# Gate/up and down projections of a SwiGLU FFN as 2x2x2 block products with seven half-size products for eight, in two phases, on Trainium2

## The chip, the cores and the metric

The kernel runs on one core of a Trainium2 chip. The metric is the device time of one execution in microseconds; the time of a kernel is the median of several runs. A profile is one execution recorded by the hardware profiler. Its engines are TensorE (PE; its weight loads are PEld), VectorE (DVE), ScalarE (ACT), GpSimd (POOL) and SyncE (SP), which issues all DMAs here.

## The reference

A hybrid decoder block on x of 1024 tokens by 1024 channels, all in fp32. The change touches only the FFN, with F = 2816:

```python
h = rmsnorm(x, g_ffn[i])
gu = h @ w_gate_up[i]                                   # (1024, 1024) @ (1024, 5632)
x = x + (jax.nn.silu(gu[..., :D_FF]) * gu[..., D_FF:]) @ w_down[i]   # @ (2816, 1024)
gate = jax.nn.sigmoid(rmsnorm(x, g_ple_gate[i]) @ w_ple_gate[i])
e = rmsnorm(p[i] @ w_ple_up[i], g_ple_post[i])
x = x + gate * e
```

Before the FFN come an RMSNorm, an input projection, a convolution branch and a pooling branch, and an output projection that is added to x; after the gate comes a final RMSNorm.

## The kernel before

**Precision.** Every fp32 operand of a matmul is split into a high part (a copy in the type fp32r) and a low part (the value minus the high part). A product of a 128x128 stationary tile with a 128x512 moving tile is three matmuls (`product`, L883 to L885): low by high, high by low, high by high, accumulated in one PSUM bank. ScalarE makes the high parts (`copy`, L579), GpSimd (L379) or VectorE (L1192) the low parts.

**Layout.** `xres` holds x as eight token tiles of 128x1024. For the FFN each tile is normalised (`normed`, L1210), turned by TensorE (`turn`, L919), and split into `act_hi` and `act_lo`, channels on the partitions, tokens along the free axis.

**FFN.** F is taken in 11 chunks of 256 columns. Per chunk TensorE computes gate and up for 2 stripes of 128 features and 2 halves of 512 tokens (64 products, k over 8 channel tiles), then down for 8 token tiles and 2 halves of 512 output columns (32 products). Between them `inner` makes silu(gate) * up: ScalarE a sigmoid (L817), VectorE two multiplications (L1354, L1358), ScalarE the high and VectorE the low part. `add_rows` (L1369) adds each finished down bank onto `xres`, which stays in SBUF all the time. The weights of a chunk come by three DMAs of 1 MB: two of gate/up in runs of 1 KB, one of W_down in runs of 4 KB.

**Order.** Each engine's instructions run in the order written; engines wait for each other only on semaphores, written out by hand. So an instruction that waits holds back all behind it on its engine. SyncE too waits, then issues, in written order. PSUM has 8 banks of 128x512 fp32; gate/up uses banks 0 to 3, down 4 to 7.

**Around the FFN.** The last output-projection rows (`rows_out`, tiles 4 to 7) alternate on TensorE with the turns of the normalised tiles; each tile goes `add_x` (L1305), square on ScalarE (L594), `rms` on GpSimd (L373, L376), `normed`, `turn`, split. After the FFN the same path is run for norm 2, then `gate_rows` multiplies by w_ple_gate, whose rows are loaded and split in the last chunk.

Of the kernel before, what the change touches and what calls it, by code (L numbers as in the profile page):

```python
# [19 lines left out]

# [10 lines left out]
P = 128  # L31
EPS = 1e-6
BANK = 512
HEADPAD = 16
DMA = 16


def hybrid_block(nc, x, p, g_mix, w_in, conv_w, conv_b, ln_g, ln_b, pool_w, pool_scale, w_out,
# [8 lines left out]
    TT = SEQ // P  # L47
# [5 lines left out]
    NCH = F // (2 * P)  # L53
    PAD = TAPS - 1
# [13 lines left out]
    e_dram = nc.dram_tensor("e_scratch", (TT, P, D), F32, kind="Internal").ap()  # L68

    with ExitStack() as ctx:  # L70
        def sb(name, shape, dt=F32):
            return ctx.enter_context(nc.sbuf_tensor(name, shape, dt))
# [36 lines left out]

        def cols_of(w, m):  # L110
# [31 lines left out]
        wd_hi = sem("wd_hi")  # L142
        wd_lo = sem("wd_lo")
# [39 lines left out]
        wo_used = sem("wo_used")  # L183
# [29 lines left out]
        PG_BANK = (4, 6, 2)  # L213
# [52 lines left out]
        def _(sp):  # L266
# [57 lines left out]
            load_gain(g_ffn[0])  # L324
            sp.wait_ge(w_lo, GU0)
            load_cols(w_gu_v, 0, F)
            for t in range(2, TT):
                sp.wait_ge(rows_added, 2 * (t - 1))
                load_x(t, raw_b[:, t % 2, :])
            sp.wait_ge(rows_added, 2 * TT)  # L330
            sp.dma_start(raw_b[:, :, :], w_dn_v[:, 0:2, :]).then_inc(rawb_in, DMA)
            sp.wait_ge(xn_ok, 2 * TT)
            load_gain(g_ple_gate[0])
            with sp.Fori(0, NCH - 1) as i:
                sp.wait_ge(w_lo, i * 4 + (GU0 + 4))
                load_cols(w_gu_v, (i + 1) * 256, (i + 1) * 256 + F)
                sp.wait_ge(wd_lo, i * 2 + 2)
                sp.dma_start(raw_b[:, :, :], w_down[0][bass.ds((i + 1) * 256, 256), :]
                             .rearrange("(f p) n -> p f n", p=P)).then_inc(rawb_in, DMA)
            sp.wait_ge(w_lo, GU0 + 4 * NCH)  # L340
            load_rows(0, w_pg_v[:, 0:2, :])
            load_rows(1, w_pg_v[:, 2:4, :])
            def load_e(t):
                sp.dma_start(e_place(t), e_dram[t]).then_inc(e_in[t], DMA)

            load_e(0)
            load_e(1)
            sp.wait_ge(wd_lo, 2 * NCH)
            sp.dma_start(raw_b[:, 0, :], g_ple_post[0].partition_broadcast(P)).then_inc(gfin_in, DMA)
            sp.dma_start(raw_b[:, 1, :], g_final.partition_broadcast(P)).then_inc(gfin_in, DMA)  # L350
            sp.wait_ge(w_lo, GU0 + 4 * NCH + 4)
# [17 lines left out]
        def _(pool):  # L369
# [153 lines left out]

            norm_2(0)
# [4 lines left out]
            split_cols(0, GU0 + 1)  # L529
            split_cols(1, GU0 + 2)  # L530
            norm_2(TT - 1)
            split_cols(2, GU0 + 3)
            split_cols(3, GU0 + 4)

            def ffn_splits(i, last):
                for f in range(2):
                    pool.wait_ge(wd_hi, i * 2 + (f + 1))
                    lo(bs_lo[:, f, :], raw_b[:, f, :], bs_hi[:, f, :], wd_lo)
                for m in range(4):
                    if last:  # L540
                        split_row(raw, m, ws_hi[:, m, :], ws_lo[:, m, :], GU0 + 4 * NCH + m + 1)
                    else:
                        split_cols(m, i * 4 + (GU0 + 4 + m + 1))

            with pool.Fori(0, NCH - 1) as i:
                ffn_splits(i, False)
            ffn_splits(NCH - 1, True)
# [29 lines left out]
        def _(act):  # L577
# [209 lines left out]
            for t in range(4):  # L787
                square_after(t, 1, 2 * t + 2)
            for n in range(KC, 2 * KC):
                scale_shift(n)  # L790
            turned_hi(0, 1)
            turned_hi(1, 1)
            square_after(4, 1, 10)
            square_after(5, 1, 12)
            turned_hi(2, 1)
            turned_hi(3, 1)
            square_after(6, 1, 14)
            turned_hi(4, 1)
            turned_hi(5, 1)
            act.wait_ge(wo_used, 1)  # L800
            for m in range(4):
                split_cols(m, 6 * DMA)
            square_after(7, 1, 16)
            turned_hi(6, 1)
            turned_hi(7, 1)


            def ffn(i, last):
                for f in range(2):
                    act.wait_ge(rawb_in, i * DMA + 3 * DMA)  # L810
                    act.wait_ge(rows_done, i * 16 + 16)
                    copy(bs_hi[:, f, :], raw_b[:, f, :], wd_hi)
                for f in range(2):
                    for h in range(HALVES):
                        s = 2 * f + h
                        act.wait_ge(gu_mm, i * 4 + (s + 1))
                        act.activation(wide[:, 0, (s % 2) * BANK:(s % 2 + 1) * BANK], ps[:, 2 * (s % 2), :],  # L817
                                       ACT.Sigmoid).then_inc(sig_ok, 1)
                        act.wait_ge(in_ok, i * 4 + (s + 1))
                        copy(bs_hi[:, 2 + f, h * BANK:(h + 1) * BANK],  # L820
                             wide[:, 1, (s % 2) * BANK:(s % 2 + 1) * BANK], in_hi)
                    act.wait_ge(gu_mm, i * 4 + (2 * f + 2))
                    for m in (2 * f, 2 * f + 1):
                        if last:
                            split_row(m, ws_hi[:, m, :], (7 + NCH - 1) * DMA)
                        else:
                            split_cols(m, i * DMA + 7 * DMA)

            with act.Fori(0, NCH - 1) as i:
                ffn(i, False)  # L830
            ffn(NCH - 1, True)

            for t in range(TT):
                square_after(t, 2, 16 * NCH + 2 * (t + 1))
                if t >= 3:
                    turned_hi(t - 3, 2)
            act.wait_ge(rows_done, 16 * (NCH + 1))

            def pg_rows(ks):
                for k in ks:  # L840
                    act.wait_ge(raw_in[k // 2], (7 + NCH) * DMA)
                    copy(bs_hi[:, k, :], raw[:, k, :], pg_hi)

            pg_rows(range(4))
            turned_hi(TT - 3, 2)
            turned_hi(TT - 2, 2)
# [33 lines left out]
        def _(pe):  # L880
            def product(dst, w_hi_, w_lo_, m_hi, m_lo, start, stop):

                pe.matmul(dst, w_lo_, m_hi, start=start, stop=False)  # L883
                pe.matmul(dst, w_hi_, m_lo, start=False, stop=False)  # L884
                return pe.matmul(dst, w_hi_, m_hi, start=False, stop=stop)  # L885
# [211 lines left out]
            rows_out(7, range(4, KD), True, False).then_inc(wo_used, 1)  # L1097
            rows_out(7, range(4), False, True)
            pe.wait_ge(rows_added, 14)
            turn(6, 1)  # L1100


            def down(i, t):
                h = t // HT
                if t % HT == 0:
                    pe.wait_ge(in_lo, i * 4 + (3 + h))
                for d in range(2):
                    n = 2 * t + d
                    pe.wait_ge(rows_added, i * 16 + (16 + n - 3))
                    for f in range(2):  # L1110
# [332 lines left out]
```

## Time and profile before

| what | value |
|---|---|
| time, median of 3 runs (lowest, highest) | 1134.55 us (1134.23, 1134.79) |
| span of the profiled execution, first to last instruction | 1132.9 us |
| TensorE matmul busy | 1093.7 us, 97% |
| VectorE / ScalarE / GpSimd busy | 519.5 / 304.8 / 365.7 us |
| DMA | 75.73 MB, mean 67 GB/s |

The span is that of the profiled execution; it lies 1.65 us below the median of the runs. A matmul's busy time covers its pipeline, so matmuls overlap one another in it; what one costs is the distance from start to start. The slices of the page show TensorE at 9 tenths or more from the second slice to the last, but for the fifth to eighth (5, 8, 9, 5).

### The profile page before, as it was taken

How to read it: one execution, taken by the hardware profiler on the slowest of the kernel's cores; microseconds unless marked ns; L12 is line 12 of the kernel's file. 1: busy time of each engine (PE TensorE's matmuls, PEld its weight loads, DVE VectorE, ACT ScalarE, POOL GpSimd, SP SyncE). 2: the span in 40 equal slices, each digit the busy share in tenths (PEclk: the TensorE clock that was granted, in tenths of full speed). 3: DMA queues.
4: the chain of work that ended last, by engine and by line, in shares of the span. 5: the costliest groups of instructions: out<-in, count | busy, mean ns of one | idle time of the engine just before them, and what ended most of it. 6: DMA issues, size and time to landing. Idle time of an engine off the chain costs nothing.

```text
span 1132.9 us, 12791 instructions
## 1 busy us (share of the span) xinstructions
PE 1093.7 (97%) x4909; PEld 905.0 (80%) x4909; DVE 519.5 (46%) x711; ACT 304.8 (27%) x430; POOL 365.7 (32%) x271
## 2 busy tenths in 40 slices
PE   5999999589999999999999999999999999999997
PEld 4888887468888888888888888888888888888885
DVE  5699799995433223241413314142331424139544
ACT  5734267213421120111112111111211111226332
POOL 4547689411242123122112213111311311231541
PEclk8999999799999999999999999999999999999999
DMA  8221204141041203021210302121030202101311
GB/s 283 82 75 38 75 11 174 75 130 56 22 164 41 72 1 112 0 74 37 71 40 0 111 0 74 37 74 37 0 111 0 75 36 111 38 26 50 130 56 74
DMA packets 44927, 75.73 MB, mean 67 GB/s; under 512 B 1585, under 2 KB 33857, under 8 KB 44896
## 3 DMA queue, kind: packets, MB, share of 16 engines
q1 hardware_dynamic: 44896, 75.31, 19.5%
q8 instruction: 20, 0.33, 0.1%
q14 instruction: 11, 0.09, 0.0%
HBM read 66.92 MB, written 8.39 MB: 66 GB/s over the span
## 4 chain that ended last, share of the span: by engine, by line
PE 86%; DVE 6%; issue 5%; ACT 1%; POOL 1%; DMA 1%; DVEq 1%; SPq 0%; POOLq 0%; ACTq 0%
PE ps L883 28%; PE ps L885 28%; PE ps L884 28%; DVE ps L1261 2%; PE ps L919 1%; DVE act_lo L1192 1%; DVE resid L1294 1%; DMA resid<-in_x 1%; DVE act_hi L1296 1%; ACT junk L594 0%; DVEq L1259 0%; POOL wide L468 0%; DVE scr L1210 0%; PE ps L979 0%; DVE resid L1267 0%
## 5 line engine op out<-in xcount | busy, mean ns | idle before, releaser
L883 PE MATMUL ps<-act_hi,ws_lo 128*128 128x512 f32 x832 | 325.9, 392 | 3.0 <-DVE act_lo L1192 2.6
L884 PE MATMUL ps<-act_lo,ws_hi 128*128 128x512 f32 x832 | 324.8, 390 | 0.0
L885 PE MATMUL ps<-act_hi,ws_hi 128*128 128x512 f32 x832 | 324.7, 390 | 0.0
L379 POOL TENSOR_TENSOR ws_lo<-raw,ws_hi 128x1024 fp32r<-128x1024 f32 x58 | 140.6, 2442 | 414.2 <-ACT ws_hi L579 414.2
L1354 DVE TENSOR_TENSOR wide<-ps,wide 128x512 f32<-128x512 f32 x44 | 30.4, 691 | 379.4 <-ACT wide L817 379.4
L883 PEld LDWEIGHTS ps<-act_hi,ws_lo 128*128 128x128 f32 x832 | 156.8, 189 | 36.0 <-issue 3.6
L885 PEld LDWEIGHTS ps<-act_hi,ws_hi 128*128 128x128 f32 x832 | 156.8, 188 | 32.8
L884 PEld LDWEIGHTS ps<-act_lo,ws_hi 128*128 128x128 f32 x832 | 156.9, 189 | 32.4
L1369 DVE TENSOR_TENSOR resid<-resid,ps 128x512 f32<-128x512 f32 x176 | 118.3, 686 | 82.2 <-PE ps L885 80.7
L883 PE MATMUL ps<-bs_hi,bs_lo 128*128 128x512 f32 x384 | 149.9, 390 | 0.1
L885 PE MATMUL ps<-bs_hi 128*128 128x512 f32 x384 | 149.4, 389 | 0.0
L884 PE MATMUL ps<-bs_lo,bs_hi 128*128 128x512 f32 x384 | 149.4, 389 | 0.0
L1261 DVE SCALAR_TENSOR_TENSOR ps<-resid,convw,ps 128x512 f32<-128x512 f32 x184 | 122.6, 745 | 0.0
L817 ACT ACTIVATE wide<-ps 128x512 f32<-128x512 f32 x44 | 26.3, 598 | 340.4 <-PE ps L885 340.4
L379 POOL TENSOR_TENSOR bs_lo<-raw_b,bs_hi 128x1024 fp32r<-128x1024 f32 x24 | 57.0, 2396 | 144.6 <-ACT bs_hi L579 144.6
L883 PEld LDWEIGHTS ps<-bs_hi,bs_lo 128*128 128x128 f32 x384 | 72.1, 188 | 15.4 <-ACT raw_b L579 0.5
L885 PEld LDWEIGHTS ps<-bs_hi 128*128 128x128 f32 x384 | 72.1, 188 | 15.0
L884 PEld LDWEIGHTS ps<-bs_lo,bs_hi 128*128 128x128 f32 x384 | 72.1, 188 | 14.8
L579 ACT ACTIVATE bs_hi<-raw_b 128x1024 fp32r<-128x1024 f32 x24 | 24.1, 1054 | 174.4 <-PE ps L885 171.6
L883 PE MATMUL ps<-ws_hi,act_lo 128*128 128x512 f32 x136 | 54.6, 401 | 13.0 <-POOL ws_lo L379 11.4
L594 ACT ACTIVATE junk<-resid 128x1024 bf16<-128x1024 f32 (+1 forms) x33 | 34.1, 1032 | 110.4 <-DVE resid L1305 63.7
L579 ACT ACTIVATE ws_hi<-raw 128x1024 fp32r<-128x1024 f32 x60 | 60.0, 1047 | 3.4 <-PE ps L885 3.4
(114 smaller groups left out, 1193.6 us busy)
## 6 DMA issues: line engine op xcount, KB each, us to landing
raw<-in_w_gate_up SPq DMA_DIRECT2D x22, 1024.0 KB, 7.4
raw_b<-in_w_down SPq DMA_DIRECT2D x11, 1024.0 KB, 4.8
resid<-in_x SPq DMA_DIRECT2D x8, 512.0 KB, 7.2
raw<-in_w_in SPq DMA_DIRECT2D x4, 1024.0 KB, 6.6
raw<-in_w_out SPq DMA_DIRECT2D x4, 1024.0 KB, 5.7
e_scratch<-raw_b SPq DMA_DIRECT2D x8, 512.0 KB, 2.6
raw_b<-in_x SPq DMA_DIRECT2D x8, 512.0 KB, 4.4
raw<-in_w_ple_gate SPq DMA_DIRECT2D x4, 1024.0 KB, 5.9
```

The lines of the kernel that those rows point to most:

```text
L379: pool.tensor_tensor(dst, src, hi.bitcast(F32), ALU.subtract).then_inc(done, 1)
L579: act.activation(dst, src, ACT.Copy, scale=scale).then_inc(done, 1)
L594: act.activation(junk[:, c], xres[:, t, c], ACT.Square, accum_out=ss[:, at:at + 1]).then_inc(ss_ok, 1)
L817: act.activation(wide[:, 0, (s % 2) * BANK:(s % 2 + 1) * BANK], ps[:, 2 * (s % 2), :], ACT.Sigmoid).then_inc(sig_ok, 1)
L883: pe.matmul(dst, w_lo_, m_hi, start=start, stop=False)
L884: pe.matmul(dst, w_hi_, m_lo, start=False, stop=False)
L885: return pe.matmul(dst, w_hi_, m_hi, start=False, stop=stop)
L919: ins = pe.transpose(ps[:, turn_bank(norm, t) + j, q * P:(q + 1) * P], xn_place(n)[:, k * P:(k + 1) * P], ident[:, :])
L1192: dve.tensor_tensor(dst, src, hi.bitcast(F32), ALU.subtract).then_inc(done, 1)
L1261: dve.scalar_tensor_tensor(out=conv_c if k == last_odd else acc, in0=resid[:, bass.ds(c * UW + (k + h * BANK), BANK)], scalar=convw[:, bas ...
L1354: dve.tensor_tensor(wide[:, 0, a], ps[:, b, :], wide[:, 0, a], ALU.mult).then_inc(gs_ok, 1)
L1369: dve.tensor_tensor(x_, x_, ps[:, 4 + n % 4, :], ALU.add).then_inc(rows_added, 1)
```

## The change

Both FFN products are written as Winograd's form of Strassen's 2x2x2 block product, in which seven half-size products and some sums replace eight. With blocks A11..A22 and B11..B22: S1 = A21 + A22, S2 = S1 - A11, S3 = A11 - A21, S4 = A12 - S2, T1 = B12 - B11, T2 = B22 - T1, T3 = B22 - B12, T4 = B21 - T2; products 1 = A11 B11, 2 = A12 B21, 3 = S4 B22, 4 = A22 T4, 5 = S1 T1, 6 = S2 T2, 7 = S3 T3.

**Phase 1, gate/up.** The token halves are the even and the odd token tiles, the k halves channels 0 to 511 and 512 to 1023, the column halves gate and up. The S forms of the activations are made once, at the hand-over (`even_lo`, `pair_forms`, `form_hi`). F is taken in 22 quads of 128 features; each quad is 7 parts of 4 products (28). For each quad VectorE makes T1 to T4 (four 128x512 subtractions), ScalarE copies and GpSimd low parts follow, and the seven parts accumulate in two banks, out of which partial sums are copied and added:

```diff
+        HEAD = ((0, 1), (0, 2), (1, 1), (1, 2), (0, 6), (0, 5), (0, 7), (0, 3), (0, 4),
+                (1, 6), (1, 5), (1, 7), (1, 3), (1, 4))
+        ORDER = HEAD + tuple((q, i) for q in range(2, QUADS) for i in (1, 2, 6, 5, 7, 3, 4))
...
+                if i == 6:
+                    pe.wait_ge(fs2_lo, 2)
+                    pe.wait_ge(t12_lo, q + 1)
+                    pe.wait_ge(p1_ok, q + 1)
+                if i == 5:
+                    pe.wait_ge(fs1_lo, 4)
+                    pe.wait_ge(c11_ok, q + 1)
+                if i == 7:
+                    pe.wait_ge(fs34_lo, 1)
+                    pe.wait_ge(t34_lo, q + 1)
+                    pe.wait_ge(u2_ok, q + 1)
+                if i == 3:
+                    pe.wait_ge(fs34_lo, 2)
+                    pe.wait_ge(wb22_lo, q + 1)
+                    pe.wait_ge(p5_ok, q + 1)
+                if i == 4:
+                    pe.wait_ge(fa_lo, 12)
+                    pe.wait_ge(c22_ok, q + 1)
```

VectorE's loop over the quads:

```diff
+            for q in range(QUADS):
+                if q:
+                    in_1(q - 1)
+                    if q % 2 == 0:
+                        in_forms(q // 2 - 1)
+                if q >= 2:
+                    c11(q)
+                if q + 1 < QUADS:
+                    t_12(q + 1)
+                if q:
+                    gs_0(q)
+                if q + 1 < QUADS:
+                    t_34(q + 1)
+                c22(q)
+                in_0(q)
```

ScalarE's:

```diff
+            for q in range(QUADS):
+                if q:
+                    sigmoid_1(q - 1)
+                    hi_t34(q)
+                if q >= 2:
+                    copy_p1(q)
+                if q:
+                    sigmoid_0(q)
+                copy_u2(q)
+                if q and q + 1 < QUADS:
+                    hi_b(q + 1)
+                copy_p5(q)
+                if q + 1 < QUADS:
+                    hi_t12(q + 1)
+                    hi_b22(q + 1)
```

GpSimd's:

```diff
+            for q in range(QUADS):
+                lo_t34(q)
+                if q + 1 < QUADS:
+                    if q:
+                        lo_b(q + 1)
+                    lo_t12(q + 1)
+                    lo_b22(q + 1)
```

`in_forms` makes the S forms of the FFN activations of two quads; SyncE stores seven forms of 128x512 per pair of quads in DRAM (`in_dram`). `xres` holds only four tiles now: after `add_x` each x tile is stored in DRAM (`x1_dram`), and the place of the others is used for the partial sums. Weights of a quad come as two DMAs of 512 KB in runs of 512 B.

**Phase 2, down.** Seven parts in the order 1, 5, 6, 3, 7, 2, 4, each over 11 steps (one per pair of quads), 77 steps of 4 products. A step loads one activation form and one W_down block of 128x512 (256 KB each, runs of 2 KB), in parts 5 and 7 a second W_down block; ScalarE makes two high parts, VectorE two low parts and in parts 5, 6, 7 and 4 one T form. The raw ring has four places, the split ring three:

```diff
+            def step_hi(n):
+                pi, i, j = e_step(n)
+                act.wait_ge(ab_in[n % 4], 2 * DMA * (n // 4 + 1))
+                if n >= 3:
+                    act.wait_ge(ed_mm, 4 * (n - 2))
...
```

VectorE's loop over the steps:

```diff
+            for n in range(3):
+                step_lo(n)
+            in_1(QUADS - 1)
+            in_forms(PAIRS - 1)
+            for n in range(3, STEPS):
+                pi, i, j = e_step(n)
+                step_lo(n)
+                if n + 2 < STEPS and E_ORDER[(n + 2) // PAIRS] in (5, 6, 7, 4):
+                    step_t(n + 2)
+                if pi and j < 4:
+                    step_sum(pi - 1, j)
```

SyncE's queue at the change of phase:

```diff
+            for n in range(4, 7):
+                load_step(n)
+            store_pair(PAIRS - 1)
+            sp.wait_ge(d_mm, len(ORDER))
+            for form in range(7):
+                sp.wait_ge(in_stored[form], DMA * PAIRS)
+            for t in EVEN_ODD:
+                sp.dma_start(xres[:, t, :], x1_dram[t]).then_inc(x_in[t], DMA)
+            for n in range(7, STEPS):
...
+                load_step(n)
```

TensorE's steps:

```diff
+            for n in range(STEPS - 3):
+                pi, i, j = e_step(n)
+                pe.wait_ge(e_lo, 2 * n + 2)
+                if n == 0:
+                    pe.wait_ge(fa_lo, 12)
+                    pe.wait_ge(gs1_ok, QUADS)
+                    pe.wait_ge(c12_ok, QUADS)
+                if j == 0 and pi >= 2:
+                    pe.wait_ge(ed_ok, 4 * (pi - 1))
+                for m in range(4):
+                    step_mm(n, m).then_inc(ed_mm, 1)
+                if pi == 6 and j in (5, 7):
+                    turn(j // 2 - 2, 2)
+            pe.wait_ge(e_lo, 2 * STEPS)
+            for m in range(4):
+                for n in range(STEPS - 3, STEPS):
+                    last = step_mm(n, m)
+                last.then_inc(ed_mm, 1)
```

**Around them.** The last output-projection tile is done in two column halves with the turn of tile 6 between them (`last_half`); the turn of an even tile now waits for `fs4_ok` (its predecessor pair's last S form), the turn of an odd tile for `fa_lo`. The w_ple_gate rows are loaded one by one and split between steps 12 and 47 of phase 2 (high parts ScalarE, low parts GpSimd). Norm 2 and `gate_rows` take the even tiles first; two turns lie in the last part of phase 2, the other six between the gate rows.

## Rows read from the trace of the kernel before

**Rows 1.** The page: span, and busy time by engine

```profile
span 1132.9 us, 12791 instructions
...
PE 1093.7 (97%) x4909; PEld 905.0 (80%) x4909; DVE 519.5 (46%) x711; ACT 304.8 (27%) x430; POOL 365.7 (32%) x271
```

**Rows 2.** A window of 100 us in the FFN: busy us (instructions) per engine, clock, DMA

```profile
400.00:500.00 100.00, 100.00 (x443) 82.81 (x442) 30.96 (x46) 17.61 (x23) 23.82 (x10) 1.00 0.15 48
```

**Rows 3.** Timeline of SyncE's DMA issues: W_down of two successive chunks

```profile
382.62 0.37 SPq L338 DMA_DIRECT2D raw_b<-in_w_down  x1
...
447.90 0.37 SPq L338 DMA_DIRECT2D raw_b<-in_w_down  x1
```

**Rows 4.** Chain of waits, 200 longest pieces: turns of tiles 4 and 5, a stall of TensorE

```profile
296.56 1.75 PE ps L919 x16
...
1034.13 0.51 issue
```

**Rows 5.** Timeline of ScalarE in one FFN chunk: start, duration, idle before and releaser

```profile
452.73 0.60 ACT L817 ACTIVATE wide<-ps 128x512 f32<-128x512 f32 x1 [8.87 <-PE ps L885]
454.81 0.63 ACT L579 ACTIVATE bs_hi<-wide 128x512 fp32r<-128x512 f32 x1 [1.48 <-DVE wide L1358]
```

**Rows 6.** Timeline of VectorE in the same chunk

```profile
453.36 0.69 DVE L1354 TENSOR_TENSOR wide<-ps,wide 128x512 f32<-128x512 f32 x1 [10.82 <-ACT wide L817]
454.08 0.69 DVE L1358 TENSOR_TENSOR wide<-wide,ps 128x512 f32<-128x512 f32 x1
455.47 0.69 DVE L1192 TENSOR_TENSOR bs_lo<-wide,bs_hi 128x512 fp32r<-128x512 f32 x1 [0.70 <-ACT bs_hi L579]
```

**Rows 7.** Page, part 5: 1024-wide splits on GpSimd and ScalarE

```profile
L379 POOL TENSOR_TENSOR ws_lo<-raw,ws_hi 128x1024 fp32r<-128x1024 f32 x58 | 140.6, 2442 | 414.2 <-ACT ws_hi L579 414.2
...
L579 ACT ACTIVATE ws_hi<-raw 128x1024 fp32r<-128x1024 f32 x60 | 60.0, 1047 | 3.4 <-PE ps L885 3.4
```

**Rows 8.** Timeline of VectorE while GpSimd works, 180 to 184 us

```profile
180.86 2.87 DVE L1294 TENSOR_TENSOR resid<-resid 128x512 f32<-128x512 f32 x1 [0.28 <-DVE resid L1267]
```

**Rows 9.** Timeline of GpSimd in the same stretch

```profile
180.75 2.42 POOL L379 TENSOR_TENSOR ws_lo<-scr,ws_hi 128x1024 fp32r<-128x1024 f32 x1
```

**Rows 10.** Timeline of VectorE at the hand-over to the FFN, 296 to 316 us

```profile
296.60 0.69 DVE L1305 TENSOR_TENSOR resid<-ps,raw_b 128x512 f32<-128x512 f32 x1 [4.69 <-PE ps L885]
...
300.19 1.28 DVE L1210 SCALAR_TENSOR_TENSOR scr<-resid,rs,gain 128x1024 f32<-128x1024 f32 x1
...
312.87 2.63 DVE L1210 SCALAR_TENSOR_TENSOR scr<-resid,rs,gain 128x1024 f32<-128x1024 f32 x1
```

**Rows 11.** Timeline of ScalarE in the same stretch

```profile
297.32 1.06 ACT L594 ACTIVATE junk<-resid 128x1024 bf16<-128x1024 f32 x1 [9.55 <-DVE resid L1305]
```

**Rows 12.** Timeline of GpSimd in the same stretch

```profile
298.83 0.55 POOL L376 TENSOR_TENSOR rs<-ss,neg_half 128x1 f32<-128x1 f32 x1
```

**Rows 13.** DMA issues by line: KB each, median us from issue to landing

```profile
raw_b<-in_w_down SPq DMA_DIRECT2D x11, 1024.0 KB, 4.8
...
e_scratch<-raw_b SPq DMA_DIRECT2D x8, 512.0 KB, 2.6
...
out_x<-scr SPq DMA_DIRECT2D x2, 256.0 KB, 2.0
```

**Rows 14.** Windows of 1 us inside transfers: 512 B, 1 KB and 4 KB runs

```profile
13.00:14.00 1.00, 0.97 (x5) 0.57 (x4) 1.00 (x2) 0.74 (x2) 0.92 (x2) 1.00 1.17 291
367.00:368.00 1.00, 1.00 (x7) 0.81 (x6) 0.69 (x1) 0.00 (x0) 0.00 (x0) 1.00 1.05 355
385.00:386.00 1.00, 1.00 (x6) 0.84 (x5) 0.00 (x0) 0.00 (x0) 0.00 (x0) 1.00 1.06 434
```

**Rows 15.** Windows of 2 us around TensorE's idle time at 239 us

```profile
240.00:242.00 2.00, 0.00 (x0) 0.00 (x0) 2.00 (x4) 0.00 (x0) 0.00 (x0) 1.00 0.00 0
244.00:246.00 2.00, 2.00 (x12) 1.82 (x11) 2.00 (x4) 0.74 (x1) 0.00 (x0) 0.50 0.00 0
246.00:248.00 2.00, 2.00 (x10) 1.85 (x9) 2.00 (x4) 1.56 (x4) 0.93 (x3) 0.66 0.82 254
```

More of the change, by code:

```diff
@@ L21 @@
+import math
 from contextlib import ExitStack
@@ L330, in _ @@
[L330 to L339, printed above, removed]
@@ L528, in _ @@
                 norm_2(t)
-            split_cols(0, GU0 + 1)
-            split_cols(1, GU0 + 2)
+            lo_b(0)
             norm_2(TT - 1)
[L532 to L547, printed above, removed]
+            lo_b(1)
+            lo_t12(0)
+            lo_b22(0)
+            for q in range(QUADS):
[5 more added lines that the diff above has]
+                    lo_b22(q + 1)
+            for k in range(KD):
+                pool.wait_ge(pg_hi, k + 1)
+                hi_, lo_ = (ws_hi, ws_lo) if k < 4 else (bs_hi, bs_lo)
+                lo(lo_[:, k % 4, :], scr[:, k % 3, :], hi_[:, k % 4, :], pg_lo)
             def e_rms(t):
@@ L797, in _ @@
+            form_hi(3)
             square_after(6, 1, 14)
[L798 to L802, printed above, removed]
-            square_after(7, 1, 16)
[L804 to L842, printed above, removed]
@@ L844, in _ @@
-            pg_rows(range(4))
-            turned_hi(TT - 3, 2)
-            turned_hi(TT - 2, 2)
+            hi_b(0)
+            form_hi(4)
+            form_hi(5)
+            form_hi(6)
+            hi_b(1)
+            square_after(7, 1, 16)
+            hi_t12(0)
+            hi_s2(0, 3)
+            copy_p1(0)
+            form_hi(7)
+            hi_s2(3, 4)
+            sigmoid_0(0)
+            copy_p1(1)
+            for i in (7, 3):
+                act.wait_ge(fs4_ok, 4)
+                copy(s_form(ws_hi, bs_hi, i), s3 if i == 7 else s4[:, :, :], fs34_hi)
@@ L848, in gate @@
+            for t in range(4, TT):
+                act.wait_ge(ed_ok, 25 + t - 4)
+                square(t, 2)
+                if t == 5:
+                    turned_hi(2, 2)
+            turned_hi(3, 2)
             def gate(t, j, c):
@@ L1330, in _ @@
+            even_lo(0)
             normed(2, 1, 2)
-            turned_lo(1, 1)
+            pair_forms(0)
             normed(3, 1, 2)
@@ L1334, in _ @@
             add_x(5)
-            for t in range(4, 6):
-                turned_lo(t - 2, 1)
-                normed(t, 1, 2)
+            even_lo(1)
+            normed(4, 1, 2)
+            pair_forms(1)
+            normed(5, 1, 2)
             add_x(6)
-            turned_lo(4, 1)
+            even_lo(2)
             normed(6, 1, 2)
-            turned_lo(5, 1)
+            pair_forms(2)
+            even_lo(3)
             add_x(7)
-            turned_lo(6, 1)
+            t_12(0)
             normed(7, 1, 2)
-            turned_lo(7, 1)
@@ L1376, in _ @@
[L1376 to L1391 removed]
+            s2_lo(0, 3)
@@ L1392, in _ @@
+            for m in range(4):
+                step_sum(6, m)
+            turned_lo(1, 2)
+            normed(2, 2, 3)
+            normed(3, 2, 3)
+            turned_lo(2, 2)
+            turned_lo(3, 2)
+            for t in range(4, TT):
+                normed(t, 2, 3)
+                if t >= 5:
+                    turned_lo(t - 1, 2)
             turned_lo(TT - 1, 2)
```

689 lines of the change are left out of this document (538 added, 151 removed).

## The prediction

> **What bounds the kernel now.** I read the page first: TensorE is busy for 97% of the span, VectorE for 46%, GpSimd for 32% [rows 1]. In a window of 100 us inside the FFN TensorE has no idle time at full clock, the other engines are busy 31, 18 and 24 us, and the DMA engines are at 0.15 [rows 2]. So in the FFN time is the number of matmuls times their distance. A chunk is 64 + 32 products of 3 matmuls, 288, and successive chunks are 447.90 - 382.62 = 65.28 us apart [rows 3]: 0.2267 us a matmul, 718 us for 11 chunks. Only two kinds of things can count: matmuls that go, and places where TensorE comes to wait.
>
> **What goes.** Gate/up had 11 x 64 = 704 products and gets 22 x 28 = 616; down had 352 and gets 77 x 4 = 308. That is 132 products, 396 matmuls, x 0.2267 = 89.8 us. Moving tiles stay 512 wide in three passes, so I leave the distance as it is; that phase 1 reads them as four runs of 128 is the one unknown in it. No row shows this form. Its bounds are nothing and, were such a matmul twice as long, 1848 x 0.2267 = 419 us, far above the gain; the turns' and down's 128-wide runs of `act_hi` as weights cost nothing that [rows 3] shows, so I take nothing.
>
> **Phase 1, steady state.** A part is 12 matmuls, 2.72 us, a quad 19.04. The unit prices: ScalarE 0.60 to 0.63 for 512 columns and 1.05 for 1024, VectorE 0.69 and 0.72 from start to start when chained, GpSimd 2.44 for 1024, hand-overs 0.2 from TensorE and 0.03 to 0.1 else [rows 5 to 7]. Per quad: VectorE 11 operations + half of `in_forms`, 13 x 0.70 = 9.1 us; ScalarE 3 x 1.05 + 6 x 0.61 = 6.8; GpSimd 3.5 x 2.44 = 8.5. All are under half of 19.04. What matters is the order. Counted from a quad's start: `sigmoid_1` 0.2 to 0.8, `hi_t34` to 1.85, so `lo_t34` 1.9 to 4.4; `copy_p1` 2.9 to 3.5 (part 6 wants it at 5.44); VectorE's `c11` at 5.65 (part 5 wants it at 8.16); `copy_u2` 8.4 to 9.0 (part 7: 10.9); `copy_p5` 11.1 to 11.7 (part 3: 13.6); `c22` 13.8 to 14.5 (part 4: 16.3). The tightest is an even quad, with `in_forms` ahead of `c11`.
>
> There the port question enters. An operation of VectorE with both inputs in SBUF, 0.69 us when GpSimd rests [rows 6], took 2.87 us when GpSimd ran a 2.42 us subtraction, and ended 0.56 us after it [rows 8, 9]; `normed` went from 1.28 to 2.63 in the same way [rows 10]. So the first operation of `in_forms`, at 2.3, is held until 4.9, the others follow to 7.1, `c11` ends at 7.8: 0.4 us before part 5 wants it. I take no loss here. (The Trainium skill, "SBUF — State Buffer", section "SBUF: two separate sides", calls the pair of ports shared by VectorE and GpSimd an exclusive lock held for the instruction; the trace agrees. By it the worst case would be a hold per GpSimd instruction.)
>
> **Hand-over to the FFN.** Before, TensorE did not wait here. The turns of tiles 4 and 5 end at 298.3 [rows 4], then `last_half(0)` (24 matmuls, 5.44) to 303.75. The turn of tile 6 needs the S4 of pair 2. ScalarE: square of tile 6 to 298.4 [rows 11], `hi_b(0)` to 299.5, high parts of tiles 4 and 5 to 301.5. VectorE: `even_lo(2)` to 301.2, `normed(6)`, held by `lo_b(0)` (299.5 to 301.9), to 303.2, four forms x 0.70 to 306.0: **2.3 us** late. Then `last_half(1)` to 312.4, parts (0,1), (0,2) to 317.9. `normed(7)` has its factor at 315.6 (square and `rms`, prices of [rows 11, 12]) but meets `lo_b(1)`: 318.3, **0.4** late. Parts (1,1), (1,2) to 324.6. VectorE: `s2_lo` of 1536 columns, 1.9 us, held behind `lo_t12(0)`, to 322.3, `c11` 323.0, four forms 325.8, the last S2 low part 326.5: **1.9** late. Parts 6 and 5 to 332.0; part 7 needs `t34_lo`: ScalarE has first the copies of S3 and S4 (2048 columns, 2.0 each), to 330.9, `hi_b22` and `hi_t34` to 332.5, GpSimd to 335.2: **3.3** late. Then `c22(0)` stands behind `t_12(1)` and `t_34(1)`: **0.4**. Sum 8.3 us; ends of the range 4 (no holding) and 14 (each of the SBUF-only operations held).
>
> **Change of phase.** Let T0 be the end of the last part. Step 0 waits for `gs1_ok`, the first half of `in_1(21)`, which VectorE reaches behind `in_0` (to -1.1) and six low parts (4.2): 3.1, + 0.7 = T0 + 3.9. Behind it come the second half (4.6), `in_forms` (7.5), the last store (2.0 to 2.6 to land [rows 13]; 9.9). Only then SyncE issues eight x tiles, 4.2 MB, 0.4 us each, and `load_step(7)` behind them in its queue. At 0.42 MB per us (runs of 4 KB gave 434 GB/s, of 1 KB 355 [rows 14]) that lands at 24.0; two high and two low parts, and step 7 starts at 26.0. Seven steps before it would be 19.04. So the change of phase costs **7.0 us** (3.9 at step 0, 3.1 at step 7); ends 3.9 (loads overtake) and 12 (x tiles at 291 GB/s).
>
> **Phase 2, steady state.** A step is 2.72 us of TensorE. VectorE: two low parts, in four of seven parts a T form, in four of eleven steps a sum: 3.36 x 0.70 = 2.35 us; ScalarE 1.3. A load has from the low parts of step n-4 to the T form of n: 10.88 - 5.4 = 5.5 us. 1 MB takes 4.8 us, 512 KB stored 2.6 [rows 13]; 512 KB loaded I take as 3.5 and 768 KB as 4.5 to 5. Bandwidth: 524 KB per 2.72 us is 193 GB/s, in parts 5 and 7 289 GB/s, against 355 to 434. It fits, with little room in 22 steps. Eight GpSimd low parts of 2.44, one per five steps, hold VectorE up to 2.2 us each: in parts 5 and 6 12.1 + 2.2 = 14.3 us of work per 13.6 us. TensorE has 3.1 us in hand per step. I take **3 us**; ends 0 and 22 x 0.9 = 20 (768 KB at the 219 GB/s that the lone 1 MB load shows over issue to landing: 3.6 us a step).
>
> **The end.** The last three steps wait for the low parts of step 76, whose high parts wait for step 73; `turned_lo(0)` is ahead of them on VectorE: **2.5 us**. The rest of the norms runs between gate rows of 5.44 us each and I find no wait; the 0.5 us at 1034 [rows 4] goes: 2.0. Ends 0.5 and 6.
>
> **The clock.** After 4.8 us of idle time at 239 the granted clock stood at 0.50, then 0.66, for some 3 us, that is 1.2 GHz and back to 2.4 [rows 15]: 1.5 us lost. The waits above are 2 to 4 us; after the one at step 0 the loss is hidden by step 7's wait. I take **2 us**, ends 0 and 6. (The Trainium skill, "TensorE: Matmul & The Clock Gate", "HAM oscillation — how this bites in real kernels", warns of exactly such gaps; that gaps of this size suffice no run here shows.)
>
> **Sum.** -89.8 + 8.3 + 7.0 + 3.0 + 2.0 + 2.0 = -67.5. From the profiled 1132.9 that is 1065.4, and with the 1.65 us to the median 1067.
>
> **Rivals.** (a) *Phase 2 is bound by its loads.* For it: 256 KB pieces, only four places, at most two steps under way, two thirds of the DMA capacity wanted. Against: two loads overlap, and windows inside transfers reach 355 and more. At 3.6 us a step in 22 steps the time is 1067 - 3 + 20 = 1084. The Trainium skill, "DMA: Bandwidth & Descriptors", "Bandwidth", advises transfers of at least 1 MiB; one after another, by its fit (2.0 us + bytes/436e3), two of 256 KB would be an estimated 5.2 us, far beyond a step. By rows, the store of 256 KB took 2.0 and of 512 KB 2.6 [rows 13]: the fixed part is 1.4 us, and if each load paid it alone, a step would be 2 x 2.0 = 4.0 us, x 77 - 209 = +99, which gives 1163, slower; the 2 MB of gate/up at 355 GB/s without a gap speaks against it. (b) *The port makes VectorE the bound of phase 1.* Place: nine SBUF-only operations per quad. If GpSimd's holding and its being held add up so that `c11` comes late in even quads by 1 us, 10 us: 1077. The gain is used up when a quad takes 67/22 = 3.1 us more; with all nine at 2.87 a quad is 9 x 2.87 + 4 x 0.69 = 28.6 us, +9.5, that is 1276, slower. Against: GpSimd works only 8.5 us of 19. (c) *The waits at the seams mostly vanish* (slack that I counted pessimistically): 4 + 3.9 + 0 + 0.5 gives 1053. (d) *Strided moving tiles are slower.* 3% on 1848 matmuls would be 12.6 us: 1080. Against: nothing in the rows; a weak case.
>
> **Chances.** Forecast, 1057 to 1078: 0.57. (a) in its mild form 0.14, as +99 us 0.02; (b) mild 0.10, severe 0.02; (c) 0.10; (d) 0.05. A measurement of this kernel tells 0.2%, 2.3 us, from no change. Faster 0.95, same 0.01, slower 0.04. The range takes in the forecast, (b) mild, (d), most of (a), and the near part of (c): 1054 to 1089.
>
> **What would show it.** Right: per quad 19.0 us in phase 1 with no idle TensorE; idle TensorE of about 4 us at the change of phase with `in_1` as releaser and about 3 us seven steps later, with the load of step 7 or its splits as releaser; 2 to 3 us at three places of the hand-over. Wrong: a distance over 0.2267 in phase 1; idle time per step in parts 5 and 7 released through raw's loads; VectorE operations of 2 us and more in many quads with TensorE waiting on `c11`; a clock below 1 over more than 10 us.

## The result, and the profile after

The changed kernel takes 1106.26 us (median of 4 runs, 1105.26 to 1108.31) against 1134.67 for the kernel before (4 runs, 1134.23 to 1134.95): ratio 0.9751, interval 0.9737 to 0.9764. It is 28.4 us faster, where 67.5 were forecast, and lies 17 us beyond the end of the range (1089).

The page of the changed kernel, to be read against [rows 1], and with TensorE's busy tenths, granted clock and the DMA's share in 40 slices of 27.6 us:

```profile
span 1103.6 us, 12625 instructions
...
PE 1022.3 (93%) x4513; PEld 841.0 (76%) x4513; DVE 738.2 (67%) x931; ACT 424.9 (39%) x636; POOL 426.3 (39%) x297
...
PE   5999999589987999999999999998887888999997
...
PEclk8999999799998999999999999998898998999999
DMA  8221203343203422334142324238765577643021
```

TensorE has 4909 - 4513 = 396 matmuls less, as counted, but its busy share has fallen from 97% to 93%. Four slices were thin before as well, the first, the eighth and ninth (5 and 8 tenths) and the last; the text on the profile before names the fifth to eighth, which is wrong. The others show where it fell: the 12th and 13th, the hand-over, and the 28th to the 34th, phase 2. Slices 14 to 27, phase 1, are full. Windows of 20 us, columns as in [rows 2]: two of the hand-over, one of phase 1, three of phase 2:

```profile
300.00:320.00 20.00, 16.83 (x82) 13.64 (x81) 15.18 (x17) 8.37 (x14) 7.23 (x5) 1.00 0.06 26
320.00:340.00 20.00, 13.22 (x52) 10.22 (x52) 19.90 (x19) 9.92 (x12) 7.64 (x3) 0.89 0.19 54
560.00:580.00 20.00, 20.00 (x90) 16.58 (x89) 12.63 (x15) 7.36 (x11) 8.86 (x4) 1.00 0.29 88
...
780.00:800.00 20.00, 16.15 (x59) 12.75 (x58) 14.06 (x21) 6.38 (x12) 2.35 (x1) 0.83 0.72 231
840.00:860.00 20.00, 15.91 (x58) 12.57 (x58) 9.83 (x13) 6.59 (x11) 2.36 (x1) 0.83 0.59 177
...
900.00:920.00 20.00, 14.73 (x63) 11.85 (x62) 14.24 (x22) 7.22 (x12) 2.35 (x1) 0.89 0.65 224
```

In phase 1 TensorE has no idle time; VectorE, at 63%, does not hold it up. The distance of the quads comes from TensorE's timeline, the first matmul of part 1 of quad 2 and that of quad 20:

```profile
361.79 0.39 PE L1217 MATMUL ps<-act_hi,wa_lo 128*128 128x512 f32 x1
```

```profile
704.51 0.39 PE L1217 MATMUL ps<-act_hi,wa_lo 128*128 128x512 f32 x1
```

(704.51 - 361.79) / 18 = 19.04 us a quad, 84 x 0.2267: the matmul distance of [rows 3], with moving tiles in four runs of 128 columns. So the 89.8 us of matmuls went as forecast. Part of them was given back by idle time. The view of waits for TensorE says who waited for whom (total us, times, longest); of its lines those that the kernel before does not have:

```profile
PE ps L1217 <- DVE ring_lo L1564: 29.1, 10, 5.3
...
PE ps L1217 <- POOL wc_lo L565: 5.6, 1, 5.6
...
PE ps L1217 <- DVE gtmp L1781: 3.4, 1, 3.4
...
PE ps L1263 <- DVE s L1725: 2.0, 1, 2.0
PE ps L1217 <- DVE ws_lo L1564: 1.2, 1, 1.2
```

and place by place in phase 2, TensorE's timeline (start, duration, in brackets the idle time before and its releaser):

```profile
746.12 0.77 PE L1217 MATMUL ps<-ring_hi,ring_lo 128*128 128x512 f32 x1 [3.37 <-DVE gtmp L1781]
...
771.58 0.50 PE L1217 MATMUL ps<-ring_hi,ring_lo 128*128 128x512 f32 x1 [3.44 <-DVE ring_lo L1564]
...
793.64 0.80 PE L1217 MATMUL ps<-ring_hi,ring_lo 128*128 128x512 f32 x1 [3.85 <-DVE ring_lo L1564]
```

The first is step 0, the second step 7, the other eight are one step each, and come every five steps. Behind a wait for VectorE's `ring_lo` there must be something that VectorE waits for, and that is seen in the waits of ScalarE from 740 us on:

```profile
ACT ws_hi L782 <- DMA scr<-in_w_ple_gate: 21.3, 4, 6.3
ACT bs_hi L782 <- DMA scr<-in_w_ple_gate: 20.8, 4, 7.5
```

ScalarE stood 42.1 us in eight places, 4 + 4, until a row of w_ple_gate had landed. One of them, ScalarE's timeline and SyncE's:

```profile
782.27 0.62 ACT L782 ACTIVATE ring_hi<-keep 128x512 fp32r<-128x512 f32 x1
788.95 1.06 ACT L782 ACTIVATE ws_hi<-scr 128x1024 fp32r<-128x1024 f32 x1 [6.06 <-DMA scr<-in_w_ple_gate]
789.91 0.61 ACT L782 ACTIVATE ring_hi<-raw 128x512 fp32r<-128x512 f32 x1
```

```profile
782.03 0.43 SPq L487 DMA_DIRECT2D raw<-in_w_down  x1
...
782.99 0.43 SPq L527 DMA_DIRECT2D scr<-in_w_ple_gate  x1
```

SyncE issues the row at 782.99, behind the load of step 15, which it may issue only when step 11's low parts are done. ScalarE wants it right after the high parts of step 12, at 782.9. It lands at 788.95. The high parts of step 13 stand behind it in ScalarE's queue, though step 13's loads were issued as early as 774.3 and 774.8 (they land in 3.0 and 3.8 us, median). They still need the place in the split ring that step 10 gives back; going by the 2.72 us between the earlier such moments, that was at about 784.4 (an estimate), so the row holds them for some 5.5 us. VectorE then waits for them, and TensorE, with step 12 in hand, runs dry.

Something else stands in the same wait. ScalarE makes the high part of the row first, so GpSimd starts its low part of the row just ahead of VectorE's low part of step 13. GpSimd's timeline and VectorE's:

```profile
790.08 2.35 POOL L565 TENSOR_TENSOR ws_lo<-scr,ws_hi 128x1024 fp32r<-128x1024 f32 x1 [62.03 <-ACT ws_hi L782]
```

```profile
790.56 2.43 DVE L1564 TENSOR_TENSOR ring_lo<-raw,ring_hi 128x512 fp32r<-128x512 f32 x1 [4.74 <-ACT ring_hi L782]
```

VectorE's operation, 0.68 us elsewhere, took 2.43 and ended 0.56 us after GpSimd's. In each of the eight places one low part is lengthened so, by about 1.7 us, which makes up to 13 of TensorE's 24.5 us of idle time there (an estimate: 1.7 in six places, and the whole of the two waits that are shorter than that).

**The account** in the profiled execution: 1132.9 - 89.8 + 9.95 (four waits at the hand-over: 1.99, 1.18, 1.20, 5.58) + 6.8 (steps 0 and 7) + 24.5 (eight rows: 3.85, 3.05, 1.50, 4.09, 1.10, 2.87, 2.74, 5.27) + 1.2 (the last three steps) - 0.5 (the wait of [rows 4]) = 1085.1. The span is 1103.6. The 18.5 us left are matmuls at a greater distance; the granted clock fits: its mean fell from 0.987 to 0.969, and (1 - 0.969) x 1103.6 - (1 - 0.987) x 1132.9 = 19.5 us of clock, some of it in idle time. Windows of 2 us say where: (1 - clock) x 2 us, summed, is 3.4 us at the hand-over, 5.1 between 744 and 776 us (behind steps 0 and 7), and 11.9 behind steps 13, 18, 28 and 48, together 20.4; it is nothing in phase 1, and nothing in the kernel before from 296 to 1128 us. Windows around the wait at step 13:

```profile
790.00:792.00 2.00, 0.00 (x0) 0.00 (x0) 1.44 (x1) 2.00 (x6) 1.92 (x1) 1.00 0.05 20
792.00:794.00 2.00, 0.36 (x1) 0.36 (x2) 2.00 (x3) 0.60 (x2) 0.44 (x1) 0.73 0.00 0
794.00:796.00 2.00, 2.00 (x6) 1.52 (x6) 2.00 (x5) 0.63 (x1) 0.00 (x0) 0.50 0.60 186
796.00:798.00 2.00, 2.00 (x6) 1.59 (x5) 2.00 (x4) 0.00 (x0) 0.00 (x0) 0.50 0.97 307
798.00:800.00 2.00, 2.00 (x6) 1.51 (x5) 1.10 (x3) 0.77 (x2) 0.00 (x0) 0.57 0.99 349
800.00:802.00 2.00, 2.00 (x10) 1.65 (x9) 1.79 (x3) 0.38 (x1) 0.00 (x0) 1.00 0.83 248
```

The clock is at its lower level, 1.2 GHz, for some 6 us after a wait of 3.85 us.

### The profile page after: what moved, and what is told of

Read it like the earlier page. It is cut to its first block and busy times, and to the rows that moved or that the text cites. A ratio compares the mean times of both kernels' runs of the same rounds, so it can differ in the third digit from the quotient of the medians.

```text
span 1103.6 us, 12625 instructions
## 1 busy us (share of the span) xinstructions
PE 1022.3 (93%) x4513; PEld 841.0 (76%) x4513; DVE 738.2 (67%) x931; ACT 424.9 (39%) x636; POOL 426.3 (39%) x297
## 5 line engine op out<-in xcount | busy, mean ns | idle before, releaser
L1217 PE MATMUL ps<-ring_hi,ring_lo 128*128 128x512 f32 x308 | 127.2, 413 | 32.5 <-DVE ring_lo L1564 29.1
L1564 DVE TENSOR_TENSOR ring_lo<-raw,ring_hi 128x512 fp32r<-128x512 f32 x132 | 99.7, 791 | 81.4 <-ACT ring_hi L782 81.3
L1218 PE MATMUL ps<-ring_lo,ring_hi 128*128 128x512 f32 x308 | 125.2, 406 | 0.0
L1219 PE MATMUL ps<-ring_hi 128*128 128x512 f32 x308 | 124.4, 404 | 0.0
L782 ACT ACTIVATE ring_hi<-raw 128x512 fp32r<-128x512 f32 x132 | 76.2, 622 | 103.1 <-PE ps L1219 91.0
L1217 PE MATMUL ps<-act_hi,bs_lo 128*128 128x512 f32 x240 | 93.6, 390 | 0.0
L1219 PE MATMUL ps<-act_hi,bs_hi 128*128 128x512 f32 x240 | 93.4, 389 | 0.0
L1218 PE MATMUL ps<-act_lo,bs_hi 128*128 128x512 f32 x240 | 93.4, 389 | 0.0
L1218 PEld LDWEIGHTS ps<-ring_lo,ring_hi 128*128 128x128 f32 x308 | 61.2, 199 | 12.7
L565 POOL TENSOR_TENSOR bs_lo<-raw_b,bs_hi 128x1024 fp32r<-128x1024 f32 x24 | 59.8, 2495 | 10.2 <-ACT bs_hi L782 10.2
L1217 PE MATMUL ps<-act_hi,ws_lo 128*128 128x512 f32 x128 | 51.7, 404 | 3.0 <-DVE act_lo L1564 2.6
```

The lines of the kernel that those rows point to most:

```text
L565: pool.tensor_tensor(dst, src, hi.bitcast(F32), ALU.subtract).then_inc(done, 1)
L782: act.activation(dst, src, ACT.Copy, scale=scale).then_inc(done, 1)
L1217: pe.matmul(dst, w_lo_, m_hi, start=start, stop=False, skip_group_check=onto)
L1218: pe.matmul(dst, w_hi_, m_lo, start=False, stop=False, skip_group_check=onto)
L1219: return pe.matmul(dst, w_hi_, m_hi, start=False, stop=stop, skip_group_check=onto)
L1564: dve.tensor_tensor(dst, src, hi.bitcast(F32), ALU.subtract).then_inc(done, 1)
```

## The experiments

**e1_pg_early.** Each row is issued four steps earlier:

```diff
-                if n - 4 in PG_STEP:
-                    k = PG_STEP[n - 4]
+                if n in PG_STEP:
+                    k = PG_STEP[n]
```

> The changed kernel with one edit: each w_ple_gate row is loaded four steps earlier (before the load of step n instead of step n + 4). Theory A: in the eight steps with such a row ScalarE stands in its queue until the row has landed (42 us in all in the trace of the changed kernel), TensorE runs dry for 24.5 us in eight places and restarts at half clock in five places of phase 2. Then the row's wait vanishes, TensorE's eight waits go to under 3 us in all, and the time falls from 1106 to 1068 to 1078. Theory B: the waits come from GpSimd's low parts, which hold VectorE's two-input operations (2.4 us each, as often as before): then TensorE's waits stay and the time stays within 5 us of 1106. Theory C: phase 2 is short of DMA bandwidth: the waits move to other steps, and the time stays above 1095.

1074.77 us (1073.16 to 1076.52; ratio to before 0.9481, interval 0.9465 to 0.9497), 31.5 us less than the changed kernel. In its trace ScalarE waits for no row, and of TensorE's eight waits 2.5 us are left:

```profile
771.13 0.80 PE L1217 MATMUL ps<-ring_hi,ring_lo 128*128 128x512 f32 x1 [6.18 <-DVE ring_lo L1564]
...
786.96 0.50 PE L1217 MATMUL ps<-ring_hi,ring_lo 128*128 128x512 f32 x1 [0.24 <-DVE ring_lo L1564]
...
802.17 0.50 PE L1217 MATMUL ps<-ring_hi,ring_lo 128*128 128x512 f32 x1 [1.20 <-DVE ring_lo L1564]
```

GpSimd makes the same eight low parts, and the transfers carry the same bytes. So bandwidth did not make those waits, nor did GpSimd's low parts by themselves; the rows' place in the queues did. VectorE is still held, as at step 18 in its timeline here:

```profile
798.62 2.90 DVE L1564 TENSOR_TENSOR ring_lo<-raw,ring_hi 128x512 fp32r<-128x512 f32 x1
```

Without the row's wait ahead of it, a hold of about 2 us reaches TensorE at most as the 0.2 to 1.2 us above. In the changed kernel it came on top of that wait. No run took the hold away and left the row where it was, so the two shares of the 24.5 us are read from the trace, not tested.

**e2_pg_late.** The same edit the other way (`n - 5`).

> The other way: each w_ple_gate row is loaded one step later than in the changed kernel. Theory A: each of the eight waits grows by about a step, 2.7 us, so 8 x 2.7 = 22 us more, and with the half clock after more of them 22 to 35: 1128 to 1141. Theories B and C: no change, within 5 us of 1106.

1133.62 us (1130.03 to 1136.6): 27.4 us more than the changed kernel, inside what theory A gave. ScalarE waits 60.5 us for the rows, TensorE 42.8 in the eight places. With the rows this late the whole change brings nothing: ratio to before 0.9991, interval 0.9979 to 1.0003.

**e3_fill.** Nine matmuls that add zero, ahead of five of the waits (an extract; the tile of zeros, `zt`, is written once by GpSimd at the hand-over, which is left out here):

```diff
+                if n in (13, 18, 28, 43, 48):
+                    pe.wait_ge(zt_ok, 1)
+                    pe.wait_ge(ed_ok, 4 * (pi - 1) + 1)
+                    for _ in range(9):
+                        pe.matmul(ps[:, E_BANKS[1 - E_SET[pi]][0], :], zt[:, :], act_hi[:, 0, 0:BANK],
+                                  start=False, stop=True, skip_group_check=True)
```

> The changed kernel with nine matmuls more (2.0 us) on TensorE ahead of each of five waits of phase 2 (steps 13, 18, 28, 43, 48), with a stationary tile of zeros, accumulated onto a bank whose sum is out already, so that nothing is changed by them. They lie inside waits that end no earlier for them. Theory: the half clock after a wait costs about 3 us each time at steps 13, 18, 28 and 48; with the idle time cut by 2 us it does not fall at 13, 18 and 28: 1106 to about 1097, with the same moments of landing. Rival: what follows a wait is slow for another reason, or the clock falls all the same: 1106 or up to 3 us more.

1108.41 us (1105.26 to 1110.69): no gain. At step 13 the fill did what it should, the idle time fell to 1.66 us and the clock stayed up:

```profile
792.00:794.00 2.00, 1.44 (x7) 0.86 (x5) 2.00 (x1) 2.00 (x4) 1.89 (x1) 1.00 0.00 0
794.00:796.00 2.00, 0.90 (x4) 0.77 (x5) 2.00 (x4) 0.34 (x2) 0.00 (x0) 1.00 0.00 0
796.00:798.00 2.00, 2.00 (x11) 1.64 (x10) 2.00 (x5) 0.31 (x1) 0.00 (x0) 1.00 0.83 287
```

But the next wait, at step 18, was 3.17 us in spite of its own 2 us of fill. It ended 41.0 us after step 7's start, 41.9 in the changed kernel: 0.8 us sooner, not 3; and the last wait, of step 74, ended 225.2 us after it for 223.0. At step 28 an idle time of 2.38 us was followed by 1.2 GHz all the same. At step 38 the clock fell after 2.52 us, where in the changed kernel it had not after 2.87. The windows give 10.2 us of clock from 770 us on for 13.6 in the changed kernel, 3.4 less; but fill and idle time from step 13 to step 48 come to 10.2 + 17.6 = 27.8 us for 24.5. So the experiment does not separate the clock's cost: time won by a faster TensorE in between is mostly lost again at the next wait.

**e4_gs1.** TensorE's wait for `gs1_ok` and `c12_ok` under `if n == PAIRS` instead of `if n == 0`.

> The changed kernel, with TensorE's wait for the last in_1 and c12 moved from step 0 to step 11, the first that writes those banks. Theory: step 7 is set by the arrival of its load behind the eight x tiles, not by TensorE; so step 0 starts about 3 us earlier, step 7 waits about 3 us or more longer (some 9 to 10 us from one cause), and the time stays within 2 us of 1106. Rival: the wait at step 0 and its half clock are worth their 3.4 + 2.5 us: 1100.

1110.53 us (1103.24 to 1111.48), 4.3 us above the changed kernel and so outside the 2 us that were named, but not at 1100. Three of the four runs lie above the changed kernel's, one below. Of the 4.3 us by which the profiled executions differ, 3.4 are there before the edit acts: the last wait of the hand-over ends at 341.16 us for 337.75. TensorE's timeline has no wait at step 0 and this one at step 7:

```profile
774.23 0.79 PE L1217 MATMUL ps<-ring_hi,ring_lo 128*128 128x512 f32 x1 [9.34 <-DVE ring_lo L1565]
```

9.3 us at one place, for 3.4 + 3.4 at two with 3.4 us lost to half clock between. Counted from the end of the hand-over, step 7 starts after 433.1 us, for 433.8 in the changed kernel, though step 0 starts 4.0 us sooner by the same count (404.4 for 408.4). So step 7 is set by something that does not depend on step 0.

**e5_x_spread.** On top of e1_pg_early, the edit of e4_gs1 and the x tiles behind step 7's load:

```diff
             store_pair(PAIRS - 1)
             sp.wait_ge(d_mm, len(ORDER))
+            load_step(7)
             for form in range(7):
                 sp.wait_ge(in_stored[form], DMA * PAIRS)
-            for t in EVEN_ODD:
-                sp.dma_start(xres[:, t, :], x1_dram[t]).then_inc(x_in[t], DMA)
-            for n in range(7, STEPS):
+            for n in range(8, STEPS):
...
                 load_step(n)
+                if n < 8 + TT:
+                    t = EVEN_ODD[n - 8]
+                    sp.dma_start(xres[:, t, :], x1_dram[t]).then_inc(x_in[t], DMA)
```

> On top of e1_pg_early: step 7's load ahead of the eight x tiles, the x tiles one per step behind the loads of steps 8 to 15, and TensorE's wait for the last in_1 at step 11. Theory: step 7 was late only by its place behind 4.2 MB of x tiles, and step 0 only by that wait. Both go (3.3 and 6.2 us of idle time in e1_pg_early), with up to 3 us of half clock; at most 2 us come back where the x tiles share the queue with the loads of part 5: 1074.8 to 1062 to 1068. Rival: step 7 is late because of DMA bandwidth and latency in all, not of the order; then the wait moves to steps 8 to 15 and the time stays above 1071.

1068.32 us (1067.27 to 1070.38; ratio to before 0.9416, interval 0.9403 to 0.9429): 6.5 us less than e1_pg_early, 0.3 us above the end of the range named and below the rival's 1071. The waits at steps 0 and 7 are gone. What came back is more than the 2 us that I named, 5.5 us in steps 10 to 17, most of it in the first of part 5 (steps 11 to 21), where each step loads three blocks and x tiles and rows share the queue:

```profile
771.95 0.50 PE L1219 MATMUL ps<-ring_hi,ring_lo 128*128 128x512 f32 x1 [0.43 <-DVE ring_lo L1567]
...
776.56 0.50 PE L1219 MATMUL ps<-ring_hi,ring_lo 128*128 128x512 f32 x1 [1.59 <-DVE ring_lo L1567]
...
781.79 0.50 PE L1219 MATMUL ps<-ring_hi,ring_lo 128*128 128x512 f32 x1 [2.21 <-DVE ring_lo L1567]
...
797.28 0.50 PE L1219 MATMUL ps<-ring_hi,ring_lo 128*128 128x512 f32 x1 [1.10 <-DVE ring_lo L1567]
```

In windows of 10 us of this run the DMA engines are full from 760 to 790 us (share 1.03, 1.04, 1.04), and those of e7_all, below, show the same. So the order made the two waits. That bandwidth gives part of them back fits, but no run separates it from the order of x tiles, rows and loads in those steps.

**e6_hand.** On top of e1_pg_early:

```diff
+            hi_b22(0)
+            hi_t34(0)
             for i in (7, 3):
                 act.wait_ge(fs4_ok, 4)
                 copy(s_form(ws_hi, bs_hi, i), s3 if i == 7 else s4[:, :, :], fs34_hi)
-            hi_b22(0)
-            hi_t34(0)
```

> On top of e1_pg_early: at the hand-over ScalarE makes the high parts of B22 and of T3, T4 of quad 0 ahead of the 2048-wide ones of S3 and S4, so that GpSimd starts its two low parts before VectorE's two long two-input subtractions instead of against them. Theory: GpSimd is held by VectorE as VectorE is by GpSimd (4.4 us for a 2.4 us subtraction), and that wait of 5.6 to 6.8 us falls to 3 to 4: 1074.8 to 1071 to 1073. Rival: the wait is set by ScalarE's 3.8 us of S copies alone; then part 7 waits for S3 instead and the time stays within 1 us.

1070.99 us (1068.6 to 1072.3; 0.9432, interval 0.9419 to 0.9446), 3.8 us less. The wait is 2.79 us and is released by `ws_lo` (S3), where it was 6.77 us, released by `wc_lo`: the rival named the next releaser rightly, but it comes 4 us sooner. In the changed kernel GpSimd's two low parts, timeline:

```profile
330.87 2.44 POOL L565 TENSOR_TENSOR wc_lo<-raw,wc_hi 128x512 fp32r<-128x512 f32 x1 [10.01 <-ACT wc_hi L782]
333.27 4.38 POOL L565 TENSOR_TENSOR wc_lo<-raw_b,wc_hi 128x1024 fp32r<-128x1024 f32 x1
```

and in e6_hand:

```profile
328.25 1.61 POOL L565 TENSOR_TENSOR wc_lo<-raw,wc_hi 128x512 fp32r<-128x512 f32 x1 [7.47 <-ACT wc_hi L782]
329.88 2.79 POOL L565 TENSOR_TENSOR wc_lo<-raw_b,wc_hi 128x1024 fp32r<-128x1024 f32 x1
```

512 columns that take 1.3 us elsewhere took 2.44, 1024 that take 2.4 took 4.38, while VectorE ran its two subtractions of 2048 columns, the second of which was held in its turn (3.35 us for 2.28). In the changed kernel's timeline of VectorE:

```profile
332.10 3.35 DVE L1564 TENSOR_TENSOR bs_lo<-s,bs_hi 128x2048 fp32r<-128x2048 f32 x1
```

Put ahead of these they took 1.61 and 2.79. They end 5.0 us sooner, at 332.67 for 337.65: 2.6 because ScalarE reaches their high parts sooner, 2.4 because they are held less. The edit moves both, so the time of the run does not tell the two apart; the durations do.

**e7_all.** e5_x_spread and e6_hand together.

> e5_x_spread and e6_hand together. Theory: the two gains lie in different stretches and add: 1059 to 1066, TensorE idle in phase 2 for less than 5 us.

1065.83 us (1064.08 to 1066.0; 0.9383, interval 0.9371 to 0.9396): 40.4 us below the changed kernel, the fastest of all and inside the range named. It is 2.5 us below e5_x_spread, so of the 3.8 us of e6_hand 1.3 are not found again. TensorE's waits over 0.15 us in phase 2 come to 6.5 us, not under 5. Its windows of 10 us:

```profile
770.00:780.00 10.00, 6.17 (x26) 4.46 (x26) 6.13 (x8) 4.00 (x6) 2.40 (x1) 1.00 1.04 396
780.00:790.00 10.00, 10.00 (x39) 8.10 (x37) 7.98 (x14) 3.14 (x6) 0.00 (x0) 0.83 1.04 375
...
860.00:870.00 10.00, 10.00 (x46) 8.29 (x45) 8.72 (x12) 4.83 (x8) 2.64 (x1) 1.00 0.83 283
```

From 770 to 780 us the DMA engines are full (1.04, 396 GB/s) and TensorE loses 3.8 us; at 0.83, in part 3, it loses nothing. From 780 to 790 the clock is 0.83, which is 1.7 us lost; e5_x_spread has 1.00 there after waits of the same length (2.21 and 2.23 us).

## Why the prediction was wrong

The terms of the forecast's sum, in us, beside the same account of the two profiled executions; the last term is what is left of the span:

| term | forecast | changed kernel | e1_pg_early |
|---|---|---|---|
| matmuls | -89.8 | -89.8 | -89.8 |
| hand-over | 8.3 | 9.95 | 11.1 |
| change of phase | 7.0 | 6.8 | 9.5 |
| phase 2, steady state | 3.0 | 24.5 | 2.5 |
| the end | 2.0 | 0.7 | 0.7 |
| the clock (what is left) | 2.0 | 18.5 | 4.4 |
| sum | -67.5 | -29.3 | -61.6 |

Of the 38.2 us between the first two sums, 21.5 are phase 2 and 16.5 the clock.

**The matmuls** (-89.8): right, to the rounding of the distance.

**Phase 1, no waits**: right. An even quad with `in_forms` was as tight as worked out, but nothing waited: in the quad that starts at 514.1 us `c11` ended 7.6 us after its start, where 7.8 were forecast. The rival (b), the port as the bound of phase 1, and (d), strided moving tiles, did not come; nor did (c), since the waits at the seams were there.

**Hand-over** (8.3 us): 9.95 us at the same four places of the forecast's five (2.3, 0.4, 1.9, 3.3, 0.4 forecast; 1.99, 1.18, 1.20, 5.58 measured, the last 0.4 not). Releasers and order were right; the price of the fourth left out that GpSimd, too, is held by VectorE, which lengthened its two low parts there by 1.1 and 2.0 us.

**Change of phase** (7.0 us, step 7 at T0 + 26.0): the mechanism was right, both waits with the named releasers, the queue order confirmed by e4_gs1 and e5_x_spread. T0 is 746.12 - 3.37 = 742.75, so step 7 came at + 28.8, and in e1_pg_early, where the two waits are 3.28 and 6.18, at + 28.75. In the forecast's own terms, with what half clock hides between the two waits, the change of phase cost 28.8 - 19.0 = 9.8 us and not 7.0. The eight x tiles took SyncE 5.0 us to issue, not 8 x 0.4 = 3.2, behind stores that were awaited at 754.4 instead of T0 + 9.9 = 752.7:

```profile
747.25 2.48 SPq L470 DMA_DIRECT2D in_scratch<-in_s  x4
754.37 5.00 SPq L521 DMA_DIRECT2D resid<-x_scratch  x8
759.41 0.64 SPq L485 DMA_DIRECT2D raw<-in_scratch  x1
```

**Phase 2, steady state** (3 us): here is the step that failed. The forecast counted for the w_ple_gate rows GpSimd's 2.44 us and what it does to VectorE, and left out the load that the row comes by. That load stands in SyncE's queue behind the load of step n + 3, which itself waits for the low parts of step n - 1, and ScalarE asks for the row right after the high parts of step n: at step 12 at the very moment of issue, against a median of 5.6 us from issue to landing. The step's own loads were checked against such a budget (5.5 us); the row's was not. The hold of VectorE that was counted, and found to have room, came on top, since the row had used that room up. It cost 24.5 us of idle time and, with what followed, the 31.5 us that e1_pg_early gave back. With this one edit the kernel is at 1074.8, inside the forecast's own range of 1057 to 1078, with hand-over, change of phase and clock each 2.4 to 2.8 us above their terms.

**Rival (a)**, phase 2 bound by its loads: not in steady state. Once the rows were early, TensorE's waits over 0.15 us in parts 6, 3, 7, 2 and 4 came to 1.1 us but for the last three steps, and the queue carried 396 GB/s where it was full. In the first steps of part 5 the idle time is about 5 us once the x tiles are loaded among them (e5_x_spread). Two loads of 256 KB, one behind the other in the queue, landed in 3.0 and 3.8 us (median) from issue, so they overlapped. (The forecast's 5.2 us for two such loads comes from a fit that the Trainium skill, "DMA: Bandwidth & Descriptors", gives in the section "Anatomy of one DMA — SWDGE (gpsimd) path", for transfers issued by GpSimd; SyncE issues all of these.)

**The end** (2.0): 1.24 - 0.51 = 0.7 us; TensorE waited 1.24 where 2.5 were forecast.

**The clock** (2 us): mis-sized, the second term that failed. 18.5 us are unaccounted for by matmuls and waits, and the granted clock agrees with them (20.4 us by windows, 11.9 of them behind four of the eight row waits). The forecast took the price from one place that lost 1.7 us [rows 15]; here the places lost 1.7 or 3.4 us each. But I can give the clock no price of its own, as the time that would come back without it: e1_pg_early, in which most of the waits are gone, has 4.4 us left in the same account, and e3_fill did not get any back by keeping TensorE at work in the waits. How much an execution without half clock but with the same waits would take is left open.

## What to carry to other kernels

When work for a later stage is slipped into a running pipeline, give its load the same check as the pipeline's own: when is it issued, behind what in its queue, how long does it take to land, and which in-order engine stands while it is awaited. Here eight loads of 512 KB, 4.2 MB beside the 46 MB of the steps' own and no more than 2.4 us of an engine each, took back 31 us of 90, and issuing them four steps earlier ended that. Here trading matmuls for sums took slack away (VectorE from 46% busy to 67%, the DMA's mean from 67 to 126 GB/s): the gain stood only while every engine in the chain kept its few microseconds in hand, and two small delays that each had room had none together.

## What the runs showed that was not expected

GpSimd's subtraction is held by VectorE's operations on two SBUF inputs as much as the other way round: 4.38 us for 2.4 and 2.44 for 1.3 in the changed kernel. (By the Trainium skill, "SBUF — State Buffer", section "SBUF: two separate sides", whichever starts first has the pair of ports for its whole instruction and the other waits; the trace agrees.) In the forecast I had counted one direction only.

The granted clock fell to 1.2 GHz after idle times of 3.05 us (changed kernel), 2.52 and 2.38 (e3_fill) and 2.23 (e7_all), and not after 2.87 (changed kernel) or 2.21 (e5_x_spread). What a wait of 2 to 4 us costs beyond itself differed from place to place, between nothing and 3.4 us.
